# Sample HGRN inside the first head: one block of a decoder layer dissolved into the next

## The reference, cut to what matters

```python
q = jax.nn.silu(qc) * (C_KDIM ** -0.5)
g = lbh + (1.0 - lbh) * jax.nn.sigmoid(fc)
...
bcum = jnp.cumsum(ft, axis=2)
o_inter = jnp.einsum('bhld,bhdv->bhlv', qt * jnp.exp(bcum), state)
diff = bcum[:, :, :, None, :] - bcum[:, :, None, :, :]
decay = jnp.exp(jnp.where(causal[:, :, None], diff, -jnp.inf))
attn = jnp.einsum('bhtd,bhtsd,bhsd->bhts', qt, decay, kt)
o = o_inter + jnp.einsum('bhts,bhsv->bhtv', attn, vt)
new_state = (jnp.exp(blast[:, :, 0])[..., None] * state
             + jnp.einsum('bhsd,bhsv->bhdv', kt * jnp.exp(blast - bcum), vt))
...
oc = oc * lax.rsqrt(jnp.mean(oc * oc, axis=-1, keepdims=True) + RMS_EPS)
```

## Time and profile before

| | us |
|---|---|
| median of 3 runs (lowest, highest) | 2016.18 (2013.58, 2021.17) |
| profiled execution, device time | 2022.11 |
| its span | 2020.4 |
| PE busy in the span | 1837.4 (91%) |
| DVE, ACT, POOL busy | 996.9, 871.4, 650.3 |

### The profile page before, as it was taken

The page is one execution under the profiler, slowest core; times in us unless marked ns, Lnnn a source line. Parts: engine busy times, 40 slices in busy tenths (PEclk is TensorE's granted clock), DMA queues, the critical chain, the costliest instruction groups (busy, mean ns, idle before and its releaser), DMA issues. The chain is left out here.

```text
span 2020.4 us, 30088 instructions
## 1 busy us (share of the span) xinstructions
PE 1837.4 (91%) x10924; PEld 1602.6 (79%) x10924; DVE 996.9 (49%) x2046; ACT 871.4 (43%) x1642; POOL 650.3 (32%) x882
## 2 busy tenths in 40 slices
PE   6999989999999999999999976368989998999998
PEld 5978879899999999999999965267778885566575
DVE  3437644225566666666665304544545465445342
ACT  4438762115555555565556211465555431111110
POOL 1002211005565555555655211044333422121110
PEclk9999999999999999999999986579989998899899
DMA  5210111231110212021111124751331274546631
GB/s 194 91 42 33 42 54 49 71 105 56 33 51 23 58 28 58 22 58 28 35 43 33 48 64 112 156 109 42 76 66 32 60 221 148 179 143 199 194 102 52
DMA packets 181773, 162.16 MB, mean 80 GB/s; under 512 B 65433, under 2 KB 168890, under 8 KB 180858
## 3 DMA queue, kind: packets, MB, share of 16 engines
q1 hardware_dynamic: 181626, 160.24, 27.9%
HBM read 116.89 MB, written 46.55 MB: 81 GB/s over the span
## 5 line engine op out<-in xcount | busy, mean ns | idle before, releaser
L49 PE MATMUL f_bank<-f_ht,f_whi 128*128 128x384 f32 (+2 forms) x1080 | 403.6, 374 | 5.7 <-DVE f_wlo L824 5.7
L50 PE MATMUL f_bank<-f_ht,f_whi 128*128 128x384 f32 (+2 forms) x1080 | 383.2, 355 | 0.0
L51 PE MATMUL f_bank<-f_ht,f_wlo 128*128 128x384 f32 (+2 forms) x1080 | 382.9, 354 | 0.0
L776 ACT ACTIVATE f_scr<-f_scr 128x384 f32<-128x384 f32 (+1 forms) x210 | 114.5, 546 | 270.4 <-POOL f_scr L562 269.7
L49 PEld LDWEIGHTS f_bank<-f_ht,f_whi 128*128 128x128 f32 x1080 | 204.9, 190 | 19.9 <-DVE f_wlo L824 6.5
L50 PEld LDWEIGHTS f_bank<-f_ht,f_whi 128*128 128x128 f32 x1080 | 205.0, 190 | 13.4 <-issue 1.7
L51 PEld LDWEIGHTS f_bank<-f_ht,f_wlo 128*128 128x128 f32 x1080 | 204.2, 189 | 13.0
L1129 PE MATMUL f_tps<-f_scr 128*128 128x128 f32 x1536 | 204.6, 277 | 2.3 <-DVE f_scr L966 2.3
L1129 PEld LDWEIGHTS f_tps<-f_scr 128*128 128x128 f32 x1536 | 193.9, 192 | 5.1 <-DVE f_scr L966 2.5
L966 DVE TENSOR_TENSOR f_scr<-f_scr 128x192 f32<-128x192 f32 (+1 forms) x210 | 101.1, 482 | 181.1 <-ACT f_scr L776 180.7
L561 POOL TENSOR_TENSOR f_scr<-f_scr 128x192 f32<-128x192 f32 (+1 forms) x210 | 134.7, 641 | 82.6 <-PE f_tps L1129 80.1
(11 more groups left out here) (382 smaller groups left out, 3655.2 us busy)
## 6 DMA issues: line engine op xcount, KB each, us to landing
f_wraw<-in_w_in SPq DMA_DIRECT2D x27, 512.0 KB, 4.0
a_raw<-zf SPq DMA_DIRECT2D x48, 256.0 KB, 4.1
zt<-f_stage SPq DMA_DIRECT2D x48, 192.0 KB, 1.8
a_k<-in_ck SPq DMA_DIRECT2D x48, 192.0 KB, 3.5
a_v<-in_cv SPq DMA_DIRECT2D x48, 192.0 KB
f_scr<-in_xp SPq DMA_DIRECT2D x16, 512.0 KB, 4.2
a_x<-in_xp SPq DMA_DIRECT2D x16, 512.0 KB, 5.0
out_y_prompt<-a_y SPq DMA_DIRECT2D x16, 512.0 KB, 2.9
```

The lines of the kernel that those rows point to most:

```text
L49: nc.tensor.matmul(out, w_hi, m_hi, start=start, stop=False)
L50: nc.tensor.matmul(out, w_hi, m_lo, start=False, stop=False)
L51: return nc.tensor.matmul(out, w_lo, m_hi, start=False, stop=stop)
L776: A(lev[i % 3][:, :n], lev[i % 3][:, :n], ACT.Exp).then_inc(S["expd"], 1)
```

## The change

`hgrn_sample` and its block go. Its tiles lie in places of `attend_project` that are not in use before head 1, its PSUM tiles in the banks `a_t`, `a_x` and `a_o`. Its steps get names (`ha` to `hs`) and stand in `attend_schedule`'s order: `ha`, `hb` and `hc` among the first four splits, the others among the units of head 0. Each engine does them in place, with the same arithmetic, but for three things. The values masked by sequence are made by ACT instead of DVE. The state updates go per head (six steps `hu`, one matmul of 512 columns and two DVE instructions of 128x512 each) instead of per sequence (eight, with six matmuls of 64 columns and two DVE instructions of 128x384 each). The outputs `ho` stand one head per unit after units 11 to 16.

The four raw loads of head 0 go to four tiles and are issued at once, with the sample loads between them. The copies of the value windows go to the end of head 0's last store, `f` of (0, 3). `load_v(1)` moves from split 5 to split 9, behind a wait for the sample results. `hgrn_over` makes each engine wait for the end of the sample work before it uses the places again. One mask scratch tile (`cnt`) moves.

```diff
-def hgrn_sample(nc, sem, io, con, zf, zt, mt):
...
             groups += [(h, i, blocks[b:b + 4]) for b in range(0, len(blocks), 4)]
-    order, made = [("s", p) for p in range(4)], 0
+    order, made = [("s", 0), ("s", 1), ("ha", 0), ("s", 2), ("hb", 0), ("hc", 0), ("s", 3)], 0
+    hgrn = {1: [("hd", 0)], 4: [("he", 0)], 6: [("he", 1)], 8: [("he", 2)], 10: [("hp", 0)]}
+    for h in range(NH):
+        hgrn[11 + h] = [("ho", h)]
+        hgrn[18 + 2 * h] = [("hu", h)]
+    hgrn[19], hgrn[21], hgrn[23], hgrn[31] = [("hq", 0)], [("hr", 0)], [("hn", 0)], [("hs", 0)]
...
+        if h == 0:
+            order += hgrn.get(k, [])
...
-        raw_in = [sem(f"a_raw_in{p}") for p in range(2)]
+        raw_in = [sem(f"a_raw_in{p}") for p in range(4)]
...
+        raw += [vals0.again().tile(f"raw{p}", [P, SEQ // 2]) for p in (2,)] + [vals0.tile("raw3", [P, SEQ // 2])]
+        raw_of = lambda n: n if n < 4 else n % 2
+        raw_count = lambda n: 32 * (1 if n < 4 else (n - 4) // 2 + 2)
...
+        h_qdb, h_vb = probs1.tile("h_qdb", [P, NB, W]), probs1.tile("h_vb", [NS, NH, NB * HD])
+        h_kk, h_qc, h_kd, h_bb, h_gg, h_qd, h_lg, h_fc = (probs1.tile("h_" + n, [P, W]) for n in ("kk", "qc", "kd", "bb", "gg", "qd", "lg", "fc"))
+        h_s, h_oc, h_gc, h_lrow = vals1.tile("h_s", [P, NB, AW]), vals1.tile("h_oc", [NS, AW]), vals1.tile("h_gc", [NS, AW]), vals1.tile("h_lrow", [NH, P])
+        h_qr, h_sq = turned.tile("h_qr", [P, W]), turned.tile("h_sq", [P, W])
+        h_lev = [turned.tile(f"h_lev{l}", [P, W]) for l in LV]
+        h_gl, h_lbl, h_small = turned.tile("h_gl", [P, NB * NH]), turned.tile("h_lbl", [P, 4, NH]), turned.tile("h_small", [NS, 3, NH])
+        h_tiny, h_rowm = turned.tile("h_tiny", [P, 1]), turned.tile("h_rowm", [NS, NB])
+        h_cut, h_kdt, h_sqo, h_attn = (scaled.tile("h_" + n, shape) for n, shape in (("cut", [P, W]), ("kdt", [NS, NH * P]), ("sqo", [NS, AW]),
+                                                                                 ("attn", [NS, NH, NS])))
+        h_vv, h_mask = outs.tile("h_vv", [NS, AW]), [outs.tile(f"h_mask{l}", [NS, NS]) for l in LV]
+        h_lp, h_tp, h_op, h_up = bank_t, bank_o, bank_x, [bank_o[:, b * 512:(b + 1) * 512] for b in range(2)]
...
+        def hgrn_over(eng):
+
+            eng.wait_ge(H["us"], BASE + NH)
+            eng.wait_ge(H["s_new"], BASE + NH)
+            eng.wait_ge(H["out"], BASE + 1)
...
             load_raw(0)
+            sp.dma_start(h_lrow[:], io["hgrn_lb_logits"].rearrange("a (h p) -> (a h) p", p=P)).then_inc(H["row_in"], 16)
             load_raw(1)
+            sp.dma_start(heads(h_fc), zf[ZFC * P:(ZFC + NH) * P, SEQ:T].rearrange("(h p) t -> p h t", p=P)).then_inc(H["f_in"], 16)
+            sp.dma_start(heads(h_qr), zf[ZQC * P:(ZQC + NH) * P, SEQ:T].rearrange("(h p) t -> p h t", p=P)).then_inc(H["q_in"], 16)
+            load_raw(2)
+            sp.dma_start(h_vv[:], zt[SEQ:T, TIC:TIC + AW]).then_inc(H["v_in"], 16)
+            load_raw(3)
+            sp.dma_start(h_s[:].rearrange("p b (h v) -> p (b h) v", v=HD),
+                         io["state_hgrn"].rearrange("b h d v -> d (b h) v")).then_inc(H["s_in"], 16)
+            sp.dma_start(h_gc[:], zt[SEQ:T, TGC:TGC + AW]).then_inc(H["v_in"], 16)
             for kind, n in order:
-                if kind == "s" and n + 2 < 4 * NH:
+                if kind == "s" and 2 <= n and n + 2 < 4 * NH:
                     sp.wait_ge(S["split"], BASE + n + 1)
                     load_raw(n + 2)
+                    if n == 3:
+                        load_v(0)
+                    if n == 9:
+                        hgrn_over(sp)
+                        sp.wait_ge(H["stored"], BASE + 32)
+                        load_v(1)
                     if n in (3, 5):
...
+                elif kind == "hs":
+                    sp.wait_ge(H["s_new"], BASE + NH)
+                    sp.dma_start(io["hgrn_sample"].rearrange("b h d v -> d (b h) v"),
+                                 h_s[:].rearrange("p b (h v) -> p (b h) v", v=HD)).then_inc(H["stored"], 16)
+                    sp.wait_ge(H["out"], BASE + 1)
+                    sp.dma_start(mt[SEQ:T, :], h_oc[:]).then_inc(H["stored"], 16)
...
+                    if (h, i) == (0, SB - 1):
+                        for name, tokens in (("v_win_prompt", slice(0, SEQ)), ("v_win_sample", slice(SEQ, T))):
+                            sp.dma_start(io[name], zt[tokens, TV:TV + AW]).then_inc(H["windows"], 16)
...
+                elif kind == "ha":
+                    act.wait_ge(H["f_in"], BASE + 16)
+                    A(h_gg[:], h_fc[:], ACT.Sigmoid).then_inc(H["sig"], 1)
+                    A(h_kk[:], h_fc[:], ACT.Sigmoid, scale=-1.0).then_inc(H["sig"], 1)
+                    act.wait_ge(H["q_in"], BASE + 16)
+                    A(h_sq[:], h_qr[:], ACT.Sigmoid).then_inc(H["sig"], 1)
+                elif kind == "hb":
+                    act.wait_ge(H["lb"], BASE + 1)
+                    A(h_lbl[:, 2, :], h_lbl[:, 1, :], ACT.Exp).then_inc(H["lb_exp"], 1)
+                elif kind == "hc":
+                    act.wait_ge(H["sig"], BASE + 1)
+                    act.wait_ge(H["lb"], BASE + 2)
+                    for h in range(NH):
+                        ins = A(heads(h_lg)[:, h, :], heads(h_gg)[:, h, :], ACT.Ln, bias=h_lbl[:, 3, h:h + 1], scale=h_lbl[:, 1, h:h + 1])
+                    ins.then_inc(H["log_g"], 1)
+                    act.wait_ge(H["gated"], BASE + 1)
+                    act.wait_ge(H["log_g"], BASE + 1)
+                    act.wait_ge(H["const"], BASE + 4 + len(LV))
+                    A(h_gg[:], h_kk[:], ACT.Ln, bias=h_tiny[:, 0:1]).then_inc(H["log_k"], 1)
+                elif kind == "hd":
+                    act.wait_ge(H["b_ready"], BASE + 1)
+                    A(h_qd[:], h_bb[:], ACT.Exp).then_inc(H["exp_b"], 1)
+                    act.wait_ge(H["dif_l"], BASE + 1)
+                    A(h_kd[:], h_kd[:], ACT.Exp).then_inc(H["exp_l"], 1)
+                elif kind == "he":
+                    act.wait_ge(H["diff"], BASE + n + 1)
+                    A(h_lev[n][:], h_lev[n][:], ACT.Exp).then_inc(H["expd"], 1)
+                    if n == 0:
+                        act.wait_ge(H["kd_turned"], BASE + 1)
+                        A(h_kdt[:], h_tp[:NS, 0:NH * P], ACT.Copy).then_inc(H["kd_copied"], 1)
+                elif kind == "ho":
+                    if n == 0:
+                        act.wait_ge(H["v_in"], BASE + 32)
+                        act.wait_ge(H["const"], BASE + hgrn_const)
+                    for b in (n,) if n < 4 else (2 * n - 4, 2 * n - 3):
+                        A(h_vb[:, :, b * HD:(b + 1) * HD], v3(h_vv[:]), ACT.Copy, scale=h_rowm[:, b:b + 1]).then_inc(H["vb_r"], 1)
+                elif kind == "hq":
+                    act.wait_ge(H["o_sum"], BASE + NH)
+                    A(h_sqo[:], h_op[:NS, 0:AW], ACT.Square).then_inc(H["squared"], 1)
...
+                elif kind == "he":
+                    hs = HALVES[LV[n]]
+                    dve.wait_ge(H["expd"], BASE + n + 1)
+                    e, q3 = hblocks(h_lev[n], hs), hblocks(h_qc, hs)
+                    V.tensor_tensor(e[:, :, hs:], e[:, :, hs:], q3[:, :, hs:], ALU.mult).then_inc(H["xlev"], 1)
+                    take(n)
...
+                elif kind == "hu":
+                    if n == 0:
+                        dve.wait_ge(H["g_last"], BASE + 1)
+                    dve.wait_ge(H["o_sum"], BASE + n + 1)
+                    decay = h_gl[:].rearrange("p (b h) -> p h b", h=NH)[:, n, :].unsqueeze(2).to_broadcast([P, NB, HD])
+                    V.tensor_tensor(h_s[:, :, hv(n)], h_s[:, :, hv(n)], decay, ALU.mult).then_inc(H["s_tmp"], 1)
+                    dve.wait_ge(H["s_tmp"], BASE + n + 1)
+                    dve.wait_ge(H["us"], BASE + n + 1)
+                    V.tensor_tensor(h_s[:, :, hv(n)], h_s[:, :, hv(n)], h_up[n % 2].rearrange("p (b v) -> p b v", v=HD),
+                                    ALU.add).then_inc(H["s_new"], 1)
...
                 elif kind == "w":
+                    if n == 0:
+                        hgrn_over(dve)
...
+                elif kind == "ha":
+                    pe.wait_ge(H["row_in"], BASE + 16)
+                    nc.tensor.transpose(h_op[:, 400:400 + NH], h_lrow[:], ident[:NH, :NH]).then_inc(H["turned"], 1)
+                elif kind == "hb":
+                    pe.wait_ge(H["q_ready"], BASE + 1)
+                    pe.wait_ge(H["gated"], BASE + 1)
+                    pairs(0, h_kk, h_qc)
+                elif kind == "hd":
+                    pe.wait_ge(H["exp_l"], BASE + 1)
+                    for h in range(NH):
+                        mm = nc.tensor.transpose(h_tp[:NS, hw(h)], h_kd[:, hn(h)], ident[:, :])
+                    mm.then_inc(H["kd_turned"], 1)
+                elif kind == "he":
+                    pe.wait_ge(H["xlev"], BASE + n + 1)
+                    pairs(n + 1, h_lev[n], h_lev[n])
+                elif kind == "ho":
+                    if n == 0:
```

(53 more changed lines are left out.)

342 lines of the change are left out of this document (101 added, 241 removed).

## The result

The changed kernel takes 1994.44 us (median of 4 runs, 1986.18 to 1996.11) beside 2014.88 us of the kernel before on the same chip (4 runs, 2011.73 to 2021.17): ratio 0.9877 with the interval 0.9845 to 0.991. The forecast of 1982 with its range of 1969 to 1996 had the direction and held the time, with 1.6 us to spare at its upper end. By the medians the gain is 20.4 us, two fifths less than the 34.5 of the sum; the interval of the ratio stands for 18 to 31 us. The profiled execution went from 2022.11 to 1996.11 us, 26.0 less, a quarter under the sum. The two gains differ because 2022.11 stands 7.2 us over the median of its kernel and 1996.11 only 1.7 over that of its own.

The account below looks back on a forecast made before the run. No engine is full in the sample block: it is a chain. 64.4 - 1.5 - 4.3 - 14.1 - 6.0 - 4.0 = 34.5 us off the median of 2016.2 gives 1982 us, range 1969 to 1996.

Parts of the forecast that it names:

- What bounds, and the block that goes: The sample block is a chain with no engine full; removing it saves 64.4 us.
- Border: Before `attend_project`: setting up the sample block's 42 semaphores there too costs 1.5 us, ends 0 and 3.
- Start: From block start to the first exponential of a unit: sample work on ACT adds 4.3 us, ends 0 and 7.
- Units 0 to 11: Head 0: rounds through all engines at `he` and `hd` empty the pipeline, adding 14.1 us, ends 9 and 18.
- Units 12 to 16: Head 0: six `ho` outputs on PE at 1.98 us each with score, plus split 5, add 6.0; ends 2 and 9.
- Units 17 to 26: Head 0: DVE binds in scalings and updates, split 6's load wait goes; 4.0 us more, ends -3 and 8.
- Gate and rest: End of head 0 and after: the gate covers the sixth update and remaining sample work; nothing added.
- Better cover: Rival, head 0: upper PE clock in `ho`, cheaper rounds and start; 20.5 us added, time 1972, chance 0.13.
- No cover at all: Rival, head 0: the chain's 50.6 us are simply spliced in; gain 12 us, time 2004, chance 0.06.
- It doesn't do what it says: Rival, head 0: updates per head save nothing on PE; changes 2 us at most, inside the forecast, no separate chance.
- Slower: Rival, head 1: PE's clock stays at its lower level, up to 72 us more, time 2054, chance 0.02.

Follow-up runs that it names:

- e2: The changed kernel with POOL's fill of `h_qdb` moved behind DVE's masks; one run, 1992.35 us.
- e3: The changed kernel with the sample's steps taken apart, each put where its input is ready, same instructions; 1973.35 us, ratio 0.9788.
- e4: The changed kernel with four of the eight state products of each output left out, so its result is incomplete; one run, 1988.29 us.
- e5: The changed kernel with eight unused PE products added before each wait of `he`; one run, 1989.35 us.
- e1: The changed kernel with no semaphore presets on PE and 45 on each of three other engines; 1991.0 us, ratio 0.9896.
- e7: The changed kernel with semaphore presets spread over five engines, 15 on PE and 30 on each other; 1992.32 us, ratio 0.9873.
- e6: The kernel before with only the four raw loads of head 0 issued at once; 2015.07 us, ratio 0.999.

## Why the prediction was right, and where its sum was off

**What bounds, and the block that goes: right.** 64.44 us left. The copy of the windows lands in 12.5 us in its new place, and the 122 us behind head 0 and all after them kept their length.

**Border: mechanism right, size off.** 3.6 us instead of 1.5, outside the ends of 0 and 3. The kernel before held two borders whose waits of SP differ, 1.9 with 10 presets on PE and 3.6 with 22. That would have priced it: 0.14 us (the difference) to 0.16 (3.6 by 22) for each of 23 more, 3.3 to 3.8 in all. I didn't ask the view of SP's waits.

**Start: mechanism right, 1.9 us short.** The copy of part 2 came 11.7 us behind the first transfer (10 to 12 forecast), with 0.65 us of waiting for its load. The term had nothing for POOL's fills. One of them, 2.65 us long, held a DVE instruction of 0.35 us for 2.52, and e2 gives 1.2 us back. The table loads were not the cause. They cost what the earlier trace rows say:

```profile
1216.28 1.28 ACT L1901 ACT_TABLE_LOAD   x1
1217.57 0.52 ACT L1901 ACTIVATE a_h_gg<-a_h_fc 128x384 f32<-128x384 f32 x1
```

ACT's copy before the load ends at 1216.26, the load ends at 1217.56 and the sigmoid starts at 1217.57, so by these rows the drain that the prediction weighed isn't there. Nor do logarithms and exponentials share one load: ACT loads a table at 1234.21, between its logarithms and the exponentials of the units.

**Units 0 to 11: right.** 15.3 us instead of 14.1. The idle times before the units 5, 7 and 9 were foretold as near 3 us and are 2.68, 3.37 and 3.37; at `hd` it is 2.39. These are 11.8 us, and the sample's own work on ACT makes most of the rest. e3 shows the cause: with the steps apart the waits are gone.

**Units 12 to 16: the largest error.** 9.6 us instead of 6.0, just past the end of 9. The bound was right: PE up to unit 16 (e4), and split 5 at the end. The price was not: 1.98 us for a unit with its output, as a value between the clock's levels. It mixed 1.55 for the output, near the upper level's 1.4, with 0.43 for the score. The rows now show 3.03 us at the lower level and 1.87 or 1.77 (e5) at the upper. With 3.03 for half of the six and 1.8 for the others the term is 14.5 + 2.2, so +8.6. Apart from that, this stretch has no one value: 11.7, 12.3, 14.7 and 16.9 us were measured for the same instructions (e5, e2, the changed kernel, e1 and e7), by where in it the clock rose.

**Units 17 to 26: right.** 2.7 instead of 4.0. There is no wait of split 6 for its load any more, DVE's two instructions of an update take 0.69 us each, and the gate hides the sixth update and the two stores. **Gate and rest: right**, 0.2.

**What was luck.** Every term but that of the units 17 to 26 was too small, two of them past their own ends, and together they missed 7.7 us. The time fell inside the range by its width, not by the sum: with the medians' gain of 20.4 us the forecast's own upper bound, 1994, was just passed.

**Rivals.** "Better cover" needed PE at its upper clock in `ho` and cheaper rounds. e5 had the first and e3 both; the changed kernel had the clock for half of the outputs only. "No cover at all" gave a gain of 12 us, the forecast 34.5. The 26.0 of the profiled pair is nearer to the forecast and the 20.4 of the medians nearer to the rival, so the total doesn't choose. The trace does: from the first transfer to the end of head 0 there are 34 us more, and about 40 if the 5.7 us are added that the raw loads give back by e6, not the chain's 50.6; and the outputs and updates were indeed not waited for one by one. "It doesn't do what it says" had the updates save nothing on PE. They did save: PE was busy 15.8 us with them before and 10.5 after, under the cover of other engines. "Slower" found no support: the 122 us behind head 0 ran at 0.90 to 0.93 in all ten profiled kernels.

## What to carry to other kernels

When a dependent chain is put among the work of other engines, each step that waits should stand in its engine's list only where its input is long ready: the same instructions added 27.9 us to head 0 in rounds and 8.6 with the steps apart, where about 7 of the 19.3 us between them are the clock's (e5). A stretch that PE bounds after a time of waits should be priced at both clock levels and the ends kept as the range, since its time depends on when the clock rises. Preset semaphores and large fills are work too, and want to be priced from rows and put where nobody waits.
